# The samples' S5 inputs as eight block-diagonal products, and the samples' ranking in six steps of the last chunk

## The reference, cut to what matters

```python
# S5 branch: 32 groups of 16 channels drive a 64-dim complex diagonal state each
bu_re = einsum('blgh,gph->blgp', ug, bb_re)      # and bu_im; the samples' S5 inputs are this for L = 1
h = complex_linear_scan(abar, bu, h0)
...
# PEER: 8 heads, two sets of 128 keys, 16 experts of 16384 for each token and head
s = einsum('chsk,hsnk->chsn', q, sub_keys)
sv, si = top_k(s, 16)
cand = sv[:, :, 0, :, None] + sv[:, :, 1, None, :]
cs, sel = top_k(cand, 16);  eidx = cidx[sel];  g = softmax(cs)
act = gelu(einsum('chkd,cd->chk', u_tab[eidx], x))
out = einsum('chk,chkd->cd', g * act, v_tab[eidx])
```

## Time and profile before

| | |
|---|---|
| median of 3 runs | 3229.94 us (3224.25 to 3232.55) |
| the profiled execution's own time | 3229.8 us |
| its span | 3227.7 us |
| its mean granted TensorE clock | 0.938 |
| busy: PE, DVE, ACT, POOL | 2731.0, 2493.7, 977.1, 1238.1 us |
| moved by DMA | 1242.28 MB, mean 385 GB/s; 1032 gathers at L693 |

### The profile page before, as it was taken

How to read it: one execution, slowest core, us unless ns; L and a number is a source line. 1 busy time by engine, 2 the same in 40 slices (tenths; PEclk the granted TensorE clock), 3 DMA queues, 4 the chain that set the end, 5 groups by cost and what they waited for, 6 DMA issues and landing times.

```text
span 3227.7 us, 31756 instructions
## 1 busy us (share of the span) xinstructions
PE 2731.0 (85%) x9312; PEld 1564.0 (48%) x9312; DVE 2493.7 (77%) x5858; ACT 977.1 (30%) x3001; POOL 1238.1 (38%) x1048
## 2 busy tenths in 40 slices
PE   7998898999978988898878989899898996665666
PEld 6874554566445545555444545566444452222122
DVE  6836888888679888887669888887767897666754
ACT  2113433232134332322134432322133442222223
POOL 0003444334343444344344443333344343545553
PEclk9999999999989999999999999999999997888789
DMA  4269999999999999999999999999999998999997
GB/s 137 89 209 391 392 420 417 408 384 418 418 418 380 410 420 420 379 417 419 419 420 400 413 419 415 375 399 378 417 396 420 419 414 323 421 407 421 422 421 329
DMA packets 200445, 1242.28 MB, mean 385 GB/s; under 512 B 27704, under 2 KB 28088, under 8 KB 67664
## 3 DMA queue, kind: packets, MB, share of 16 engines
q0 software_dynamic: 148608, 1082.20, 81.6%
q1 hardware_dynamic: 50160, 153.21, 12.5%
q10 hardware_dynamic: 1504, 4.85, 0.4%
HBM read 1235.62 MB, written 4.55 MB: 384 GB/s over the span
## 4 chain that ended last, share of the span: by engine, by line
DMA 40%; PE 28%; DVE 19%; ACT 3%; issue 3%; POOL 2%; DVEq 2%; ACTq 1%; SPq 0%; POOLq 0%
DMA arena<-in_uv,arena 39%; PE psum L1816 14%; DVE arena L1464 9%; PE psum L1717 8%; DVE arena L1057 4%; DVE arena L1049 3%; ACT arena L734 3%; POOL arena L693 2%; PE psum L1861 2%; PE psum L1873 1%; DVE arena L1305 1%; PE psum L1732 1%; ACT L734 1%; PE psum L1698 1%; PE psum L1752 1%
## 5 line engine op out<-in xcount | busy, mean ns | idle before, releaser
L693 POOL DMA_INDIRECT arena<-in_uv,arena x1032 | 1234.2, 1196 | 1962.0 <-PE psum L1816 1355.1
L1816 PE MATMUL psum<-arena 128*128 128x512 f32 x3192 | 1602.6, 645 | 436.1 <-ACT arena L734 399.4
L1464 DVE CUSTOM_DVE_ANT_0 arena<-arena 128x1024 f32<-128x1024 f32 x1024 | 1239.3, 1225 | 509.9 <-DMA arena<-in_uv,arena 476.4
L1816 PEld LDWEIGHTS psum<-arena 128*128 128x128 f32 x3192 | 619.0, 202 | 1268.1 <-issue 613.8
L734 ACT ACTIVATE arena<-arena 128x128 f32<-128x128 f32 (+3 forms) x2481 | 699.5, 314 | 1602.4 <-DVE arena L1464 1436.9
L1717 PE MATMUL psum<-arena 128*128 128x256 f32 (+1 forms) x2688 | 627.0, 389 | 10.1 <-DVE arena L1057 6.4
L1717 PEld LDWEIGHTS psum<-arena 128*128 128x128 f32 x2688 | 517.9, 194 | 142.9 <-issue 69.5
L1057 DVE SCALAR_TENSOR_TENSOR arena<-arena 128x1024 f32<-128x1024 f32 (+6 forms) x461 | 373.1, 816 | 66.0 <-ACT arena L734 34.9
L1049 DVE TENSOR_TENSOR arena<-arena 128x256 f32<-128x256 f32 (+10 forms) x832 | 284.6, 382 | 23.5 <-issue 1.3
L734 ACT ACTIVATE arena<-psum 128x256 f32<-128x256 f32 (+7 forms) x266 | 107.2, 414 | 563.9 <-PE psum L1717 482.0
L734 ACT ACT_TABLE_LOAD x113 | 145.0, 1283 | 3.9 <-PEq L2131 0.8
(11 more groups left out here) (99 smaller groups left out, 1026.1 us busy)
## 6 DMA issues: line engine op xcount, KB each, us to landing
arena<-in_w_in SPq DMA_DIRECT2D x112, 512.0 KB
arena<-in_w_q SPq DMA_DIRECT2D x68, 512.0 KB
arena<-in_w_ab SPq DMA_DIRECT2D x40, 512.0 KB
arena<-in_w_out SPq DMA_DIRECT2D x34, 512.0 KB, 9.1
arena<-in_uv,arena POOLq DMA_INDIRECT x1032
arena<-in_keys SPq DMA_DIRECT2D x17, 256.0 KB, 7.5
arena<-in_w_glu SPq DMA_DIRECT2D x16, 256.0 KB
arena<-in_x_tok SPq DMA_DIRECT2D x8, 512.0 KB
```

What stands on the lines that cost most here:

```text
L693: pool.indirect_dma_start(uvring[:, r], None, i_["uv"], bass.IndirectOffsetOnAxis(column, 0)).then_inc(uv_in[r], 16)
L1464: V.tensor_tensor_reduce(out=u, in0=u, in1=hn[i // (SLOT // 2)], scale=1.0, scalar=0.0, op0=ALU.mult, op1=ALU.add, accum_out=dots_[:, b % ...
L1816: ins = mm(PV[:, half], dg[:, PAIR * (b % 2) + k], uvring[:, place(c, i) % UV, at:at + 512], start=(i % (SLOT // 2) == 0), stop=(pe_slots( ...
```

## The change

The samples' channels are copied by ACT, in the last chunk after the U projections are evicted, into `uDiag`: four blocks of 8 columns on a diagonal of 32-partition blocks, zero elsewhere. POOL clears it at the start, so `CONSTS` is 11. One product of full height with 32 columns then gives four blocks at once: 8 products with one wait ahead of them (`smp_in`) and one signal. The ranking of the samples is taken apart into its six pieces, which DVE does after its steps 36 to 41 (`RANK_AT` = 36) of the last chunk's own loop; ACT's exponential comes after its step 40. The DMA of the scores is started where it was.

```diff
-CONSTS = 10
+CONSTS = 11
+RANK_AT = OWN + 4
...
+        uDiag = Arena(arena, R.at).take(QT, 4 * NS)
...
+            pool.memset(uDiag, 0.0).then_inc(const_ok, 1)
...
+                if last:
+                    act.drain()
+                    for r in range(4):
+                        rows = slice(32 * r, 32 * r + 32)
+                        af(uDiag[rows, :, NS * r:NS * r + NS], uS[rows, :, C:N], ACT.Copy).then_inc(smp_in, 1)
...
-                    soft(lists(CH), NS * HEADS, 1)
...
-                if s == SB_AT:
+                if s == RANK_AT + 4:
+                    soft(lists(CH), NS * HEADS, 1)
+                elif s == SB_AT:
...
-                dve.wait_ge(smp_mm, 4)
+                dve.wait_ge(smp_mm, 1)
...
-                if last:
-                    dve.wait_ge(s8_in, 16)
-                    for _ in topk(lists(CH), NS * HEADS, 1, lambda t: g8[0:NS * HEADS], lambda t: i8[0:NS * HEADS]):
-                        pass
-                    dve.sem_inc(i8_ok, 1)
...
+            ranking = topk(lists(CH), NS * HEADS, 1, lambda t: g8[0:NS * HEADS], lambda t: i8[0:NS * HEADS])
             for s, _ in enumerate(batches(CH - 1, OWN, BC + 5, None), OWN):
-                if s == SB_AT:
+                if RANK_AT <= s < RANK_AT + 6:
+                    if s == RANK_AT:
+                        dve.wait_ge(s8_in, 16)
+                    next(ranking)
+                    if s == RANK_AT + 5:
+                        dve.sem_inc(i8_ok, 1)
+                elif s == SB_AT:
...
-                    for r in range(4):
-
-                        if r:
-                            pe.wait_ge(smp_mm, r)
-                        for part in range(2):
-                            for j in range(r, SJ, 4):
-                                at = NS * (SJ * part + j)
-                                ins = mm(SB[0][:, at:at + NS], wT[32 * r:32 * r + 32, QT * (2 + part) + j // 4],
-                                         uS[32 * r:32 * r + 32, j // 4, C:N], start=True, stop=True)
-                        ins.then_inc(smp_mm, 1)
+                    pe.wait_ge(smp_in, 4)
+                    for part in range(2):
+                        for q in range(QT):
+                            at = NS * (SJ * part + 4 * q)
+                            ins = mm(SB[0][:, at:at + 4 * NS], wT[:, QT * (2 + part) + q], uDiag[:, q], start=True, stop=True)
+                    ins.then_inc(smp_mm, 1)
```

More of the change, by code:

```diff
@@ L434, in build @@
         gS, accS, acS, wS = (R.take(HEADS) for _ in range(4))
+        w8 = R.take(HEADS, NS)
         mk, mk2 = R.take(NS), R.take(NS)
-        w8 = R.take(HEADS, NS)
         qT0 = uvring[:, UV - 2, 0:2 * P].rearrange("p (a b) -> p a b", a=2)
@@ L488, in build @@
         z_ok = sem("z_ok")
-        smp_mm = sem("smp_mm")
+        smp_in, smp_mm = sem("smp_in"), sem("smp_mm")
         a_ok = sem("a_ok")
```

## The result

The changed kernel takes 3248.8 us (median of 22 runs, 3224 to 3287), the kernel before 3229.1 us (22 runs, 3224 to 3237). The ratio is 1.0048, with a 95% interval of 1.0035 to 1.006, without two runs of the changed kernel, at 3283 and 3287 us, that count as slow. It is slower by half a per cent, where 3206.1 us and a gain were forecast, and the scatter of the runs in the ratio has grown from 13 to 41 us. The profiled execution took 3254.4 us.

What follows compares the result with a forecast made beforehand. The kernel was taken as bound by a stream of 1032 gathers, with edits priced in dry DMA time. Gains of 6.9 (S5 products) and 16.8 us (ranking) took 3229.8 to 3206.1 us, range 3200 to 3219.

Steps and rivals of the forecast that it cites:

- two dry places: Gather stream short of work at 2238 to 2256 us (7.9 us lost) and 2704 to 2728 us (18.7 us lost).
- The S5 products: Samples' input products on PE: 64 records become 16, taking 1.9 us; gain 6.9 us, ends 4 and 7.9.
- second rival: The stall by the S5 products moves to the GLU, half of 7.9 us stays: 3209.1 us; chance 0.08.
- 1.0 us left for it: Part of the 7.9 us gap at the S5 products left ungained because the count is tight.
- The ranking: Spread over DVE's steps 36 to 41, it fits beside the stream: gain 18.7 - 1.9 = 16.8 us.
- third rival: Steps 36 to 41 overfill DVE; at worst all 9.0 us of ranking become dry time: 3215.1 us; chance 0.08.
- The copies on ACT: Four small copies and a drain at the last chunk's start, about 1 us: cost nothing, at most 1 us.
- I take 1.9 us: Cost of the ranking's 16 stores beside a full stream, from 17.7% of the engines' 10.5 us.
- the state stores: Nearest case under load, 2590 to 2632 us: 2265 packets beside 2332 of the gathers, mean still 419 GB/s.
- The first rival: The ranking's little stores slow gathers to 67 GB/s for 17.3 us, costing 14.5 us: 3218.7 us; chance 0.20.
- The last rival: Slower: each 4-byte store holds the gather packet beside it, 168 us in all: about 3374 us; chance 0.04.
- the 61 packets: From 2718.5 to 2726 us, 61 packets took 81% of the engines' time; 1.6 us each against 0.28.

Runs made afterwards that it cites:

- s5_only: The changed kernel with the ranking put back in one go, S5 products as changed: 3223.1 us, ratio 0.9974.
- no_stores: The changed kernel without the 16 stores of indices and weights and the two loads behind them: 3204.4 us, ratio 0.9916.
- held: The kernel before, neither edit in it, with the 16 stores held back until DVE's step 60 of the last chunk: 3323.3 us, ratio 1.027.
- padded: The changed kernel with its 4-byte stores' scratch elements 512 bytes apart, loads picking words up one by one: 3207.3 us, ratio 0.992.
- spaced: The changed kernel with the 16 stores in eight pairs, eight DVE steps (some 40 us) between pairs: 3297.8 us, ratio 1.0197.
- wide: The changed kernel with scratch stored as whole 64-byte rows and read word by word, plus 16 stores of 64-byte elements: 3209.7 us, ratio 0.993.

## Why the prediction was wrong

**What held.** That the stream of gathers is the bound, and what its two dry places were worth: the kernel without the stores takes 3204.4 us, and the sum without its term for them is 3229.8 - 6.9 - 18.7 = 3204.2. That two numbers meet to 0.2 us is in part luck, with runs that lie 6 us apart. The S5 products: 6.9 us forecast, 8 measured (s5_only; 5 to 12 by its interval), with 1.97 us for the 16 records against 1.9, and without the dip after the GLU that the second rival expected. Whether the 1.0 us left for it was needed lies within that interval. The ranking: DVE did its pieces between the dots in steps 36 to 41 with the stream at 418 GB/s, so the third rival is out, and the wait for the scores is gone. Between the medians of s5_only and no_stores lie 18.7 us, the sum's term for it before the stores. The copies on ACT, the new wait of PE and the clearing on POOL cost nothing that shows.

**What failed** is one term: "I take 1.9 us" for the 16 stores. It measured 44 us in the window up to 2860 and 50 between the profiled executions; with that the sum gives 3204.2 + 44 to 50 = 3248 to 3254 us, where the kernel is. Three steps led to it. The first is the measure itself: both edits were priced in time in which the DMA engines run dry, and the 46 us went while their share stood at 1.02. The second is the price, the stores' own share of the engines' time, and that share is as small after the change (2.8% of 120 us): what they cost stands in the gathers' packets. The third is that the state stores were taken as the nearest row. They were the nearest in number and load, not in kind: taken one by one from the trace, the pieces that they write have 12 bytes and more. The nearer row was at hand: the 7.5 us in which the gathers crept at 67 GB/s right behind these very stores. It was given to the rivals and not to the sum, and held shows that the stores made 5.8 us of that dip.

**The first rival** had the right cause and too small a price. It let the gathers run at 67 GB/s for 17.3 us, the time the stores take alone. Beside a full stream they took 126 us, at a mean of 258 GB/s. Its escape, that stores which advance packet by packet with the gathers build no backlog, does not help: in the change 2161 small packets went with 4237 of the gathers', about as dense as in padded's quiet stretch (697 with 1440), and in spaced 256 stores alone were enough for a loss. **The last rival** is the one that came true in direction, though its sign, gathers below 67 GB/s for longer than 20 us, was not seen. Its point of decision was 25.6 us for all stores together, and 46 us is beyond it. Its mechanism, a price on the gather packets, is what the queues show, but on a few of them and not on each. Its price, 168 us from the 61 packets, was too high, and it had a chance of 0.04. (Its 3374 also keeps the 1.9 us in; without them it is 3372.) It spread the stores over 16 engines, which padded's pace corrects to 8. The Trainium skill states how many (DMA: Bandwidth & Descriptors, section Why a DMA increments its semaphore by 16 and not by 1): the largest number up to 16 that divides the slowest dimension of both sides, here 8 partitions. The 4.35 us of a store in padded agree.

**The rules weighed.** The Trainium skill has transfers under 512 B done as read-modify-write (the same page, Specifications). If that alone were dear, every one of these stores would be. padded and wide, with 4 and 64 bytes, lose next to nothing, so width below 512 bytes by itself is not what costs here; whether it has a part in the conflict of neighbouring words, no run shows. The turn by packets of 9 to 17 descriptors (the Trainium skill, same page, Queues, rings and completion order) does not show in padded's quiet stretch, which advances one for one on the engines that carry the stores. Its first 4 us, with 456 words to 199 gather packets, leave room for it.

**The scatter.** The stores are also what makes the time of the change vary: with them the runs of the ratio lie between 3224 and 3265 us, without them or with the words at least 16 bytes apart within 9 us in each run of four.

**Open.** Why the price of the same 16 stores is 46 us in the change, 90 in spaced and 99 in held was not settled. The stores met other steps of the loop in each. The chip of the runs may differ too, but the kernel before has a median of 3229 to 3233 us beside each of the three. What behind the engines makes neighbouring words conflict was not tried beyond the spacing, and nothing here shows it.

## What to carry to other kernels

Where one DMA stream is the bound, ask two things of every transfer that an edit moves into it: what it takes of the engines, and what it does to the packets beside it. Price it by the row that writes to the same place in the same way, even where that row is short. A stall can be the shelter of something: before closing one, list what runs in it. The small results that are turned around in DRAM were better stored here as whole rows and picked up word by word than scattered word by word: that gave 3206 to 3210 us, 0.7 to 0.8% faster than the kernel before. Scattering the words 16 bytes apart or more did as well (3206 to 3209 us).

## What was not expected of the hardware

Stores of 4 bytes whose places in DRAM lie 4 bytes apart cut a full stream of 8 KB gathers from 419 to 258 GB/s for over 100 us; 8 bytes apart to 379 or 329; from 16 bytes apart to 410 or more, as if they were not there. 2048 stores of 64 bytes, 128 bytes apart and 2 KB apart within one store, did no harm (408 GB/s from 2740 to 2860, 3209.7 us), nor did 2048 reads of 4 bytes (409). And 256 words at once were enough to bring the stream down to 66 GB/s for 5 us. The loss hardly shows in the stores' own packets (2.8% of the engines' time), nor in the typical packet of the gathers, whose median stays at 0.31 us: it lies for the most part in the 7.6% of their packets that take more than 1 us. And it reaches, by the estimate from spaced, engines that carry no store.
